# Retention heads: the two key units are accumulated in the output's banks instead of the accumulators' second turn

## The reference, cut to what matters

```python
proj = h @ w_in                       # 1024 -> q, k (256 a head), v, g (512 a head)
q = apply_rope(q, cos, sin)
k = apply_rope(k, cos, sin) * (RET_QK_DIM ** -0.5)
scores = einsum(q, k) * decay         # per head
o = rms_norm_f32(scores @ v, gn_g)    # per head, over its 512 values
o = o * silu(g)
out = o @ w_out
```

## Time and profile before

| | |
|---|---|
| median of 3 runs | 2048.06 us (2046.82 to 2049.55) |
| profiled execution, its own time | 2050.88 us |
| its span in the trace | 2048.8 us |
| mean granted TensorE clock | 0.951 |
| PE busy | 1895.2 us, 93% of the span |
| POOL busy | 1095.4 us, 53% |
| DVE busy | 815.0 us, 40% |
| ACT busy | 459.6 us, 22% |

### The profile page before, as it was taken

One profiled execution on the slowest core, in us unless ns is written; L12 is line 12 of the kernel. 1 busy time (PEld: TensorE's weight loads), 2 busy tenths in 40 slices (PEclk: granted clock), 3 DMA queues, 4 the chain that ended last, 5 costly groups with the idle time before them and its releaser, 6 DMA issues.

```text
span 2048.8 us, 27217 instructions
## 1 busy us (share of the span) xinstructions
PE 1895.2 (93%) x9694; PEld 1574.0 (77%) x9694; DVE 815.0 (40%) x1413; ACT 459.6 (22%) x933; POOL 1095.4 (53%) x856
## 2 busy tenths in 40 slices
PE   3699999999799999999999899989799779999998
PEld 3588887887688888888878677877777658887886
DVE  4615143254423333332341585885333563202300
ACT  2211112010112222212220126545213322101200
POOL 2254555557454454444356458864064467767762
PEclk8699999999799999999999899989899989999999
DMA  8322222236322322222223322100021123333331
GB/s 292 123 83 67 72 77 77 82 128 205 113 84 61 90 81 81 81 67 74 73 77 92 83 66 62 52 21 21 8 89 54 37 82 96 99 92 92 93 102 41
DMA packets 276218, 172.72 MB, mean 84 GB/s; under 512 B 5760, under 2 KB 269760, under 8 KB 274112
## 3 DMA queue, kind: packets, MB, share of 16 engines
q1 hardware_dynamic: 269136, 148.92, 24.9%
q10 hardware_dynamic: 7024, 23.02, 3.2%
HBM read 169.69 MB, written 2.10 MB: 84 GB/s over the span
## 4 chain that ended last, share of the span: by engine, by line
PE 82%; DVE 12%; ACT 2%; issue 2%; DMA 1%; POOL 1%; DVEq 0%; ACTq 0%; POOLq 0%
PE acc L370 18%; PE acc L372 17%; PE acc L371 17%; PE acc L392 3%; PE st L405 3%; PE acc L393 3%; PE acc L394 3%; PE sc L1326 2%; PE ob L1272 2%; PE sc L1306 2%; DVE ada_acc L1977 2%; DVE conv_out L2100 2%; PE bc L438 2%; DVE hn L486 1%; DMA x_tok<-in_x 1%
## 5 line engine op out<-in xcount | busy, mean ns | idle before, releaser
L676 POOL TENSOR_SCALAR wh<-raw 128x1024 fp32r<-128x1024 f32 x232 | 255.0, 1099 | 784.2 <-PE acc L372 480.7
L679 POOL TENSOR_TENSOR wl<-raw,wh 128x512 fp32r<-128x512 f32 x464 | 645.8, 1412 | 19.4
L370 PE MATMUL acc<-hh,wh 128*128 128x512 f32 x1120 | 460.4, 411 | 42.3 <-DVE ang L1906 13.9
L372 PE MATMUL acc<-hh,wl 128*128 128x512 f32 x1120 | 446.2, 398 | 0.0
L371 PE MATMUL acc<-hl,wh 128*128 128x512 f32 x1120 | 445.1, 397 | 0.0
L370 PEld LDWEIGHTS acc<-hh,wh 128*128 128x128 f32 x1120 | 216.1, 193 | 95.7 <-issue 42.8
L372 PEld LDWEIGHTS acc<-hh,wl 128*128 128x128 f32 x1120 | 215.6, 192 | 47.2
L371 PEld LDWEIGHTS acc<-hl,wh 128*128 128x128 f32 x1120 | 217.1, 194 | 45.0 <-issue 2.2
L370 PE MATMUL acc<-Yh,wh 128*128 128x512 f32 x512 | 204.3, 399 | 5.5 <-DVE xT L555 5.5
L371 PE MATMUL acc<-Yl,wh 128*128 128x512 f32 x512 | 203.6, 398 | 0.0
L372 PE MATMUL acc<-Yh,wl 128*128 128x512 f32 x512 | 203.3, 397 | 0.0
(11 more groups left out here) (386 smaller groups left out, 2693.7 us busy)
## 6 DMA issues: line engine op xcount, KB each, us to landing
raw<-in_att_w_in SPq DMA_DIRECT2D x64, 512.0 KB, 4.0
raw<-in_mlp_w SPq DMA_DIRECT2D x64, 512.0 KB, 4.0
raw<-in_ret_w_in SPq DMA_DIRECT2D x48, 512.0 KB, 3.8
ada_w<-in_ada_w ACTq DMA_DIRECT2D x8, 1536.0 KB, 8.2
raw<-in_w_in SPq DMA_DIRECT2D x23, 512.0 KB, 3.7
ada_w<-in_ada_w SPq DMA_DIRECT2D x8, 1024.0 KB, 16.5
raw<-in_ret_w_out SPq DMA_DIRECT2D x16, 512.0 KB, 4.0
raw<-in_att_w_out SPq DMA_DIRECT2D x16, 512.0 KB, 3.9
```

The source lines that it names most:

```text
L370: e.matmul(bank[:, :], wh[:, s, k, :], rhs_high(k), start=(start and k == 0), stop=False)
L372: last = e.matmul(bank[:, :], wl[:, s, k, :], rhs_high(k), start=False, stop=(stop and k == k1 - 1))
L676: e.tensor_scalar(wh[:, s, :, :], raw[:, s, :, :], 1.0, 1.0, ALU.mult, ALU.mult).then_inc(high_done, 1)
L679: low = e.tensor_tensor(wl[:, s, k0:k0 + KT // 2, :], raw[:, s, k0:k0 + KT // 2, :], wh[:, s, k0:k0 + KT // 2, :].bitcast(F32), ALU.subtract)
```

## The change

Unit 2 is accumulated in `ob0` and unit 3 in `ob1`. On PE they no longer wait for the copies of units 0 and 1 but for `r_oc2` and `r_oc3` of the head before, the last copies out of these two banks. The value units, which go to the accumulators next, now wait for the copies of units 0 and 1 in place of 2 and 3. ACT reads the four units from `acc0`, `acc1`, `ob0`, `ob1`, in the same order and behind the same waits. Nothing else differs; the instructions are the same in number and size.

```diff
@@ ScalarE, ret_scalar @@
                 for j, dst in enumerate((q_[:, 0, :], q_[:, 1, :], k_[:, 0, :], k_[:, 1, :])):
                     e.wait_ge(unit_used, c + j + 1)
-                    e.activation(dst, acc[j % 2][:, :], ACT.Copy).then_inc(*AC.done(f"r_qk{j}"))
+                    e.activation(dst, (acc + ob)[j][:, :], ACT.Copy).then_inc(*AC.done(f"r_qk{j}"))
@@ TensorE, ret_tensor @@
                 for j in range(4):
-                    e.wait_ge(*(V.at(f"r_g{j + 2}", i - 1) if j < 2 else AC.at(f"r_qk{j - 2}", i)))
-                    feat(e, acc[j % 2], c + j, U["ret"] + j, inputs="n0" if j == 0 else None)
-                tok(e, c + 4, U["ret"] + 4, "r_v0", [AC.at("r_qk2", i), AC.at("r_qk3", i)])
+                    e.wait_ge(*(V.at(f"r_g{j + 2}", i - 1) if j < 2 else AC.at(f"r_oc{j}", i - 1)))
+                    feat(e, (acc + ob)[j], c + j, U["ret"] + j, inputs="n0" if j == 0 else None)
+                tok(e, c + 4, U["ret"] + 4, "r_v0", [AC.at("r_qk0", i), AC.at("r_qk1", i)])
```

## The result

| | before | after |
|---|---|---|
| median, first comparison | 2048.64 us (2046.82 to 2049.55, 4 runs) | 2022.9 us (2022.12 to 2025.3, 4 runs) |
| profiled execution | 2050.88 | 2023.65 |
| its span | 2048.8 | 2021.6 |
| mean granted clock | 0.951 | 0.958 |

Later comparisons gave the same kernel 0.9898 (0.9878 to 0.9917) and 0.9901 (0.9887 to 0.9916). The forecast of 19.95 in 2048.06 is a ratio of 0.9903, outside the first interval and inside the other two.

What follows compares the result with a forecast made beforehand. PE bounds the kernel, standing in each head before unit 2 for ACT's copy: 12.0 us of pauses plus 7.9 of half-speed matmuls, 19.95 in all. All other terms were zero: 2048.06 - 19.95 = 2028.1 us, range 2024.0 to 2033.0.

Steps and rivals of the forecast that it cites:

- The forecast of 19.95: Four heads, unit 1's last matmul to unit 3's first: 19.95 us saved, 12.0 of pauses and 7.9 of half-speed matmuls.
- The wait removed: PE before units 2 and 3: pauses and slow clock go, 6.41, 4.52, 4.49 and 4.53 us by head.
- The waits added and moved: Units 2 and 3 find their banks free 23 us early; value units have 7.8 or 6.9 us to spare; no cost.
- the ring: Weight splits are asked for sooner: nothing taken, at most one slow split uncovered, 1.9 us once.
- The banks: Writing ob instead of acc costs nothing; rival of a slow stretch at each bank change, 2055.8 us, chance 0.01.
- After the heads: Later stages come 20 us earlier as a block; clock effect taken as zero, 3.5 to 5.2 us either way.
- The prediction's own sign: Prediction is wrong if the end of the output product hasn't come forward by the same 20 us.
- The range: Whole kernel: 2024.0 (two stretches gained, 3.5) to 2033.0 us (two lost, one slow split, 5.4); some 0.84.
- The base: Starting time of the sum: 2048.06 us, the median of the runs shown, 2.8 below the profiled execution.
- The chances: Forecast 0.86, only the pause 0.06, half given back 0.05, no change 0.02, slower 0.01; faster together 0.97.
- the rivals: Only pauses return 2036.1 (0.06); later stages give back half 2038 (0.05); wait moves 2048 (0.02); slower 2055.8 (0.01).

Runs made afterwards that it cites:

- e1: Changed kernel with its four banks, but units 2 and 3 wait again for the copies of units 0 and 1: 2044.83 us, ratio 0.9997.
- e2: Kernel before, two banks, ACT's copies of units 0 and 1 waiting only for the tail's second tile: 2031.46 us, ratio 0.9931.
- e11: Changed kernel with only unit 2 in an output bank, unit 3 staying in the second accumulator: 2025.67 us, ratio 0.9905.
- e5: Kernel before, run again without edit for a second trace: 2046.92 us, ratio to itself 1.0.
- e9: Kernel before with 15 filling identity matmuls in pauses ahead of the sparse attention's slow stretch, two waits exchanged: 2041.32 us, ratio 0.9979.
- e6: Changed kernel with 4 more 128x512 matmuls (0.91 us) on PE behind the last head: mean 2027.5 us over 4 runs.
- e14: Changed kernel with 4 more 128x512 matmuls behind the last head, measured again on one chip: mean 2026.4 us over 5 runs.
- e3: Changed kernel with 88 more 128x512 matmuls (20.0 us) behind the last head, later stages in their old place: 2045.58 us, mean 2044.5.
- e13: Changed kernel without edit, run beside delayed versions on one chip: mean 2024.8 us over 4 runs.

## Why the prediction was right, and where it was wrong

**The wait removed: right.** 20.05 us in the two first traces against 19.95, from the same four places. e1 shows that the wait alone makes the loss, e2 that it can be shortened without another bank, e11 that unit 2's wait was all of it. One of the four sizes is not fixed, though. The second to fourth head are over the pace by 4.5 us each in all four traces that have the wait (before, e1, e5, e9), but the first head by 6.41, 6.29, 8.39 and 8.38: its pause ends 2.1 us behind the end of DVE's sums (87.51 and 89.64 us in the first trace, 88.19 and 90.32 in e5), however early PE is done with unit 1. By these traces the wait was worth 19.8 to 21.9 us, and the forecast had read one of the two smaller values.

**The waits added and moved: right.** `r_oc2` and `r_oc3` were met long before, the value units had 7.7 us to spare, the ring kept up; no line for them in the list of waits.

**The banks: right.** No gap at any of the changes of bank, and the clock at 1.00 over all heads. In the kernel that the Trainium skill describes ("TensorE: Matmul & The Clock Gate", section "A second HAM failure mode: psum-queue depth-cycling"), PE idles for an instant between groups of matmuls as it cycles through the banks, and its clock goes up and down. This trace doesn't agree: the step over a change of bank is 0.22 to 0.23 us, as within a bank, and the 332 us of the heads are at 1.00.

**After the heads: this step failed, in its size.** I took zero for the clock of the later stages and bounded it by two or three half-speed stretches of 1.73 us, the price of the one that I had measured. One later stretch was not of that size: in the sparse attention some 20 us at half speed in the kernel before and some 7 in the changed one, and in the first pair of traces it cost 51.63 - 45.70 = 5.9 us by itself. With 3.1 us from the output product and 1.8 given back elsewhere, the later stages gave 7.2 us in that pair of traces, not at most 5.2. The prediction's own sign shows it as early as the output product: its end came forward by 538.71 - 515.59 = 23.1 us and not by the 20 of the heads. That this is in the main chance of the execution, and no gift of the change, is what e6 and e14 show for the sparse attention, and e3 in its mean. Both traces of the kernel before have the long stretch, but e1, which has the same pauses in the heads, had the part done in 44.43 us.

**The range: one stretch short at its low end.** Its ends were not worked out exactly: 2028.1 - 3.5 is 2024.6 and 2028.1 + 5.4 is 2033.5, where 2024.0 and 2033.0 were written. More to the point, the text bounded the clock by "two or three" stretches and the range took two; with three its low end is 2022.9, the median that was measured. It was given a chance of 0.84 and the first comparison fell out of it.

**The base: off too.** The sum was taken from a median of three runs, 2048.06. Over 81 runs the median is 2045.9. The three had fallen in the slower part of a distribution 13 us wide, and their own spread of 2.7 us had told nothing of that. From 2045.9 the same sum gives 2025.9; the median of after over 14 runs is 2024.5. Put together, the 5.2 us by which the first result missed are 2.2 of base, 1.6 of luck in the first four runs of after (2022.9 against 2024.5), and 1.4 that the larger samples still leave. Median against median, the change is worth 21.4 us. The heads alone differ by 20.4 to 21.6 between the two traces of before and the three of after, which may be most of these 1.4, and the output product by 1.5 to 3.1. Whether the change has any effect on the later stages beyond chance is open.

**The chances: right in kind.** Faster had 0.97. None of the rivals came about; the clock turned up where I had put it, in the output product and later, but on the other side.

## What to carry to other kernels

An accumulator that is freed by a copy which waits for something else entirely, here a tail in memory shared with the copy's target, is freed by that something; another idle bank for one unit is enough to step over it. Before bounding what TensorE's clock may do in the stages that a change doesn't touch, look for the longest slow stretch in the trace and count what it would be worth to have or not to have it: that, and not the price of the nearest one, is the width of the range. And three runs that agree don't show how wide a kernel's times lie when its clock is drawn in each execution.

## What the runs showed of the hardware that I had not expected

PE needs no long pause to lose its clock, and being busy doesn't bring it back at once. In the sparse attention's part PE was busy for 19.41 of 23.59 us at 2.4 GHz, in matmuls of 128 and 64 columns with pauses of 0.6 to 1.7 us, and fell to 1.2 GHz at their end. In e13 it then stayed at 1.2 GHz for 14.50 us in which it was busy for 14.50. In the first trace of the same kernel it was back after some 7 us, in e1, e2 and e14 after 3.4. With the pauses filled by 15 small matmuls of no use, so that PE was busy for 22.97 of 23.55 us, the part was 44.1 to 44.8 us long in four of four executions and the changed kernel 3.8 us faster on the mean (2020.2 against 2024.0, with a standard error of 0.7). Why the clock stays down so long while PE is busy was not settled.
